# Moving value-tile copies ahead of the second head squares on ScalarE, with two loads and two VectorE steps in another order

## The reference

```python
for l in range(DEPTH):                     # DEPTH = 2
    mod = silu(c) @ w_ada[l] + b_ada[l]    # six rows of 1024: shifts, scales, gates
    h = rms_norm(x, norm_mix[l]) * (1 + sc1) + sh1
    gq, gk, gv, ga, gr, sq, sk, sv, mix_a, mix_b = split_columns(h @ w_in[l])
    y_gla = gla_branch(gq, gk, gv, ga, gr, ...) @ w_up_gla[l]
    y_swa = swa_branch(sq, sk, sv, ...) @ w_up_swa[l]
    x = x + g1 * ((sigmoid(mix_a) * y_gla + sigmoid(mix_b) * y_swa) @ w_out[l])
    h2 = rms_norm(x, norm_ffn[l]) * (1 + sc2) + sh2
    x = x + g2 * moe_ffn(h2, w_router, b_router, w_gate[l], w_up[l], w_down[l])

# in swa_branch: each head of q and k is normalised over its 64 numbers, then rotated
q = partial_rope(rms_norm(q, qn_gain), positions)
k = partial_rope(rms_norm(k, kn_gain), positions)
# in gla_branch: decays from a low-rank product; v is used as it comes out of the projection
log_a = log_sigmoid(a_low @ w_alpha2 + b_alpha) / GLA_TAU
```

## Time and profile before

| | |
|---|---|
| profiled execution | 1449.55 us |
| its span, first to last instruction | 1447.9 us |
| median of three runs | 1445.5 us |
| PE busy | 1342.6 us, 93% |
| PEld busy | 1079.4 us, 75% |
| DVE busy | 1032.0 us, 71% |
| ACT busy | 723.7 us, 50% |
| POOL busy | 312.9 us, 22% |
| chain that ended last, by engine | PE 72%, DVE 10%, DMA 7%, DVEq 4%, ACT 4% |
| mean granted TensorE clock | 0.974 of full |

### The profile page before, as it was taken

The page is one execution under the profiler, slowest core; times in us unless marked ns, Lnnn a source line. Parts: engine busy times, 40 slices in busy tenths (PEclk is TensorE's granted clock), DMA queues, the critical chain, the costliest instruction groups (busy, mean ns, idle before and its releaser), DMA issues.

```text
span 1447.9 us, 18728 instructions
## 1 busy us (share of the span) xinstructions
PE 1342.6 (93%) x6887; PEld 1079.4 (75%) x6888; DVE 1032.0 (71%) x1035; ACT 723.7 (50%) x770; POOL 312.9 (22%) x263
## 2 busy tenths in 40 slices
PE   4979999999999999999949999999999999999993
PEld 3756777786777888888748787688788788888682
DVE  5476476667477999999981558543548999999494
ACT  5225255222236777777652536522225777777370
POOL 1000000000214444555220000000022444454130
PEclk9999999999999999999979999999999999999997
DMA  9565602677677999999842230212356899999575
GB/s 333 200 235 188 243 1 73 210 284 250 232 291 250 372 383 387 389 376 380 310 138 69 107 109 9 74 62 113 121 206 244 291 369 372 373 374 388 211 262 194
DMA packets 157546, 342.96 MB, mean 237 GB/s; under 512 B 16998, under 2 KB 19258, under 8 KB 157474
## 3 DMA queue, kind: packets, MB, share of 16 engines
q1 hardware_dynamic: 139280, 316.82, 60.4%
q0 software_dynamic: 16304, 25.05, 4.8%
q10 hardware_dynamic: 1890, 0.15, 0.1%
HBM read 351.73 MB, written 23.63 MB: 259 GB/s over the span
## 4 chain that ended last, share of the span: by engine, by line
PE 72%; DVE 10%; DMA 7%; DVEq 4%; ACT 4%; issue 1%; ACTq 0%; SPq 0%; POOLq 0%
PE PS L1254 13%; PE PS L1256 12%; PE PS L1255 12%; PE PS L1668 8%; PE PS L1672 8%; PE PS L1662 8%; DMA ring<-in_w_ada 3%; ACT reg L1003 2%; PE PS L1650 2%; DVE reg L1863 2%; PE PS L1182 2%; DVEq L2181 1%; DVE ring_parts L1933 1%; DMA ring<-in_w_in 1%; DMA ring<-in_w_out 1%
## 5 line engine op out<-in xcount | busy, mean ns | idle before, releaser
L1254 PE MATMUL PS<-ring_parts 128*128 128x512 f32 (+1 forms) x704 | 276.9, 393 | 24.0 <-ACT reg L961 12.2
L2328 DVE TENSOR_TENSOR ring_parts<-ring,reg_parts 128x2048 fp32r<-128x2048 f32 x124 | 278.1, 2283 | 3.4 <-ACT reg_parts L1105 3.4
L1105 ACT ACTIVATE reg_parts<-ring 128x2048 fp32r<-128x2048 f32 x124 | 230.3, 1909 | 62.6 <-DMA ring<-in_w_down 38.3
L1933 DVE TENSOR_TENSOR ring_parts<-ring,ring_parts 128x2048 fp32r<-128x2048 f32 (+1 forms) x52 | 112.9, 2209 | 124.3 <-ACT ring_parts L925 124.2
L1254 PEld LDWEIGHTS PS<-ring_parts 128*128 128x128 f32 x704 | 134.2, 191 | 67.8 <-issue 31.7
L925 ACT ACTIVATE ring_parts<-ring 128x2048 fp32r<-128x2048 f32 (+1 forms) x52 | 93.4, 1846 | 159.3 <-DMA ring<-in_w_in 118.7
L2328 DVE TENSOR_TENSOR ring_parts<-ring,hT_parts 128x2048 fp32r<-128x2048 f32 x68 | 155.1, 2286 | 14.5 <-issue 13.2
L1255 PE MATMUL PS<-hT_parts,ring_parts 128*128 128x512 f32 x384 | 150.4, 392 | 0.0
L1256 PE MATMUL PS<-ring_parts 128*128 128x512 f32 x384 | 150.2, 391 | 0.0
L1105 ACT ACTIVATE hT_parts<-ring 128x2048 fp32r<-128x2048 f32 x68 | 126.5, 1909 | 25.4 <-DMA ring<-in_w_gate 19.4
L1672 PE MATMUL PS<-ring_parts,reg_parts 128*128 128x512 f32 x528 | 130.6, 389 | 0.0
(11 more groups left out here) (337 smaller groups left out, 2406.2 us busy)
## 6 DMA issues: line engine op xcount, KB each, us to landing
ring<-in_w_up SPq DMA_DIRECT2D x32, 2048.0 KB, 17.1
ring<-in_w_gate SPq DMA_DIRECT2D x32, 2048.0 KB, 12.2
ring<-in_w_down SPq DMA_DIRECT2D x32, 2048.0 KB, 18.7
ring<-in_w_ada SPq DMA_DIRECT2D x40, 1024.0 KB, 6.1
ring<-in_w_in SPq DMA_DIRECT2D x16, 2048.0 KB, 7.9
ring<-in_w_out SPq DMA_DIRECT2D x4, 2048.0 KB, 8.8
reg<-y_rows SPq DMA_DIRECT2D x16, 512.0 KB, 6.2
ring<-in_w_ada SPq DMA_DIRECT2D x3, 2048.0 KB, 17.2
```

What stands on the lines that cost most here:

```text
L1105: act.activation(high[:, cols], ring[:, 3 * k + part, cols], ACT.Copy).then_inc(w_hi[part], 1)
L1254: pe.matmul(out_, left[0], right[0], start=first, stop=False)
L1933: tt(ring_r[:, unit_slot(n), cols], w, ring_r[:, 2 + n % 2, cols].bitcast(F32), ALU.subtract).then_inc(lo_done, 1)
L2328: tt(ring_r[:, 3 * k + part, cols], ring[:, 3 * k + part, cols], high[:, cols].bitcast(F32), ALU.subtract).then_inc(w_lo[part], 1)
```

## The change

In both layers ScalarE squares the first two token tiles, copies the four value tiles, squares the second two, copies `aT`, and takes the root after that. In layer 0 VectorE sums half 6 ahead of the key unit's low part, and half 7 between the two reductions; in layer 1 there are no sums, and the reductions stand as before. The key unit's load is issued ahead of halves 4 and 5 in layer 0.

```diff
-    IN_HALVES, IN_BEHIND = (2, 4, 2, 4, 4), (2, 2, 0, 1, 1)
+    IN_HALVES, IN_BEHIND = (2, 4, 2, 4, 4), (2, 4, 0, 1, 1)
...
                 act.drain()
-                for i in range(2):
-                    if i == 1:
-                        act.wait_ge(qss_done, at(qss_done, l, 1))
+
+                def square_heads(i):
                     act.activation(sqt, qk[:, 2 * i:2 * i + 2, :, :].rearrange("p t h d -> p (t h d)"), ACT.Square).then_inc(qsq_done, 1)
-                act.wait_ge(qss_done, at(qss_done, l, 2))
-                act.activation(qss[:, :, :], qss[:, :, :], ACT.Sqrt, scale=1.0 / HD, bias=eps).then_inc(qsq_done, 1)
+
+                square_heads(0)
                 for t in range(NT):
                     act.wait_ge(v_ready, at(v_ready, l, t + 1))
                     act.activation(v[:, t, :], PS[:, in_bank(Q_V + t), :], ACT.Copy).then_inc(v_done, 1)
+                act.wait_ge(qss_done, at(qss_done, l, 1))
+                square_heads(1)
                 act.wait_ge(a_ready, at(a_ready, l, 1))
                 act.activation(aT, PS[0:GLA_RANK, in_bank(Q_A), :], ACT.Copy).then_inc(a_done, 1)
+                act.wait_ge(qss_done, at(qss_done, l, 2))
+                act.activation(qss[:, :, :], qss[:, :, :], ACT.Sqrt, scale=1.0 / HD, bias=eps).then_inc(qsq_done, 1)
                 split_high(4)
...
                 sum_own(0, 1)
                 split_low(2)
-                sum_own(2, 3, 4, 5)
+                sum_own(2, 3, 4, 5, 6)
                 split_low(3)
-                sum_own(6, 7)
-
-
-                for i in range(2):
+
+                def sum_head_squares(i):
                     dve.wait_ge(qsq_done, at(qsq_done, l, i + 1))
                     dve.tensor_reduce(qss[:, 2 * i:2 * i + 2, :], sqt.rearrange("p (t h d) -> p t h d", t=2, h=NN), AX.X, ALU.add).then_inc(qss_done, 1)
+
+                sum_head_squares(0)
+                sum_own(7)
+                sum_head_squares(1)
                 dve.wait_ge(qsq_done, at(qsq_done, l, 3))
                 dve.reciprocal(qss[:, :, :], qss[:, :, :])
```

## The result

The changed kernel took 1439.52 us (median of 17 runs, 1436.15 to 1443.89), beside 1447.7 us for the kernel before in its 17 runs (1445.24 to 1452.43). The ratio is 0.9938, with a 95% interval of 0.9926 to 0.9950: by the ratio 9.0 us faster, between 7.2 and 10.7, and by the two medians 8.2 us. The forecast was 1434.7 us with a range up to 1438.5, so the time lies 1.0 us above the range. The direction is right. The gain is smaller than the 10.8 us forecast, and the kernel before itself now stands 2.2 us above the 1445.5 that the forecast started from.

What follows compares the result with a forecast made beforehand. TensorE, busy 93% of the span, was taken as the bound, with a 12.2 us layer 0 wait for ScalarE's value copies. Saving 10.8 us there and 0 in layer 1 took 1445.5 to 1434.7 us, range 1432.0 to 1438.5.

Steps and rivals of the forecast that it cites:

- What bounds: Layer 0: TensorE's 12.2 us wait for ScalarE's value copies goes, and the key unit's low part is late next.
- When the low part is ready: VectorE, layer 0: key unit's low part ends at 102.0, so TensorE's first key tile starts after a 2.8 us gap.
- the unit's landing: Layer 0 key unit's load: asked for at 76.0, lands 7.76 us later, at about 83.8.
- The fixed delay: Loads of the halves: 2.5 us of fixed delay on top of about 2.6 us of transfer for 1 MB.
- A gap of 2.8 us is shorter than both, so I take full speed.: First key tile, layer 0: gap below the 4.9 and 3.5 us preceding earlier clock falls, so the tile takes 5.7 us.
- the first rival: Clock falls in the short gap before layer 0's first key tile: price 1.4 us, giving 1436.1 us; chance 8%.
- The sum: Whole kernel: -10.8 us in layer 0 and 0 in layer 1, from 1445.5 to 1434.7 us.
- the bound of 100.3: Layer 0: low part's end if transfers share and the unit does not delay the halves; gain 12.5 us.
- The order of the queue: SyncE's loads, layer 0: served in ring order, key unit first in full, half 4 landing at 86.4 rather than 84.7.
- W_R and the decay products: Layer 0: W_R lands at 117.0 as before; TensorE's second W_R tile keeps 2.8 us of margin behind the decay product.
- Layer 1: Reciprocal 6.6 us later, but L2001 already waited 3.91 us for ScalarE; cost nothing, with 0.5 us to spare.
- The level: Absolute starting time: the difference was taken from the median of 1445.5 us, not the profiled execution's 1449.55.

Runs made afterwards that it cites:

- gap_filled_14: Changed kernel with 14 spare 128x128 products in TensorE's gap ahead of layer 0's first key tile; ratio to the kernel before 0.9923.
- queue_undone: Changed kernel with the key unit asked for behind halves 4 and 5, as before; ratio to the kernel before 0.9946.
- half4_held: Changed kernel with SyncE waiting in layer 0 until the key unit has landed before issuing half 4; ratio to the kernel before 0.9933.
- act_only: Kernel before with ScalarE's new order alone, queue and VectorE order as before; ratio to the kernel before 0.9956.
- change_again: The changed kernel run once more, unaltered, as a gauge of run-to-run time; ratio to the kernel before 0.9921.
- sums_undone: Changed kernel with VectorE's order as before: low part behind half 5, halves 6 and 7, then both reductions; ratio to the kernel before 0.9918.
- halves_later_15: half6_behind with TensorE taking halves 8 to 14 one tile later in layer 0, half 15 with 14 behind the third gate tile; median 1435.1 us, ratio 0.9905.
- half6_behind: Changed kernel with half 6 summed behind the key unit's low part and the first reduction; ratio to the kernel before 0.9942.
- half6_behind_filled: half6_behind with 14 spare products in TensorE's wait for half 8; ratio to the kernel before 0.9928.
- gap_filled: Changed kernel with 26 spare 128x128 products in TensorE's gap ahead of layer 0's first key tile; ratio to the kernel before 0.9956.

## Why the prediction was wrong

- **What bounds.** Right. The value copies no longer hold TensorE; the low part is late next; removing half 6 from in front of it removed the wait.
- **When the low part is ready.** Mis-sized by 1.1 us. Counted from W_V's issue I had 39.5 and it was 40.7. The term that failed is the unit's landing: 7.76 us from a single row, against 9.0. The fixed delay and 2.6 us for a megabyte, the sums of 3.0 and 3.2 us, half 6's landing (5.0 us instead of 5.1) and the low part's 4.49 held. The gap was 4.0 us instead of 2.8.
- **"A gap of 2.8 us is shorter than both, so I take full speed."** This step failed, and it is the first rival, given 8%, that came, with the gap of nearly 4 us that it named. The clock fell and the tile took 7.3 us instead of 5.7: 1.6 us (gap_filled_14). The reasoning was faulty beyond the size. I compared the length of the gap with the time from the last matmul to the fall, but in the changed kernel the fall came 4.9 us after the last matmul, as in the earlier trace rows, when the gap was already over. Nor is that time fixed: it was 2.3 us in queue_undone, 2.7 in half4_held, 3.2 in act_only and 4.6 in change_again. act_only and sums_undone show falls behind waits of 2.5 and 1.8 us. What a gap of just 2.8 us with a full tile behind it would have done, no run shows. The Trainium skill, page "TensorE: Matmul & The Clock Gate", section "HAM oscillation — how this bites in real kernels", describes waits for loads behind which the matmuls start at the slow clock. The trace agrees with that for the wait of 4.0 us. The waits of its example are longer than 2.8 us, so the page alone did not decide the step; the runs do.
- **The sum.** 10.8 less 1.1 and less 1.6 is 8.1, and the stretch gained 8.05. The total's interval of 7.2 to 10.7 holds this and just excludes 10.8. Two small slips of the working change nothing: the bound of 100.3 and half a microsecond of spread give 1432.5, not 1432.0, and the key unit's own 2 MB took 5.3 us of its 10.26, not 5.4.
- **The order of the queue.** The rule of the Trainium skill, page "DMA: Bandwidth & Descriptors", section "Queues, rings and completion order", was the side I took. The trace agrees: half 4, issued 3.5 us behind the unit, landed 2.7 us behind it and 8.25 us after its own issue, where it took 5.1 with nothing ahead of it.
- **W_R and the decay products.** Right in effect. W_R took 11.5 us to land instead of 10.3 and, counted from W_V's issue, landed 2.8 us later than I had it. The decay product ended at 137.1 and TensorE's second gate tile began at 140.3, without a wait. The margin of 3.1 us was no thinner than the 2.8 forecast only because TensorE came 2.7 us later as well; halves_later_15, where TensorE is earlier, waits here.
- **Layer 1.** Right:

```profile
807.51 0.40 DVE L1974 RECIPROCAL qss<-qss 128x40 f32<-128x40 f32 x1 [0.40 <-ACT qss L966]
...
822.61 1.23 DVE L2006 TENSOR_TENSOR reg<-reg 128x1024 f32<-128x1024 f32 x1 [0.91 <-ACT reg L977]
```

  L2006 still waits for ScalarE, 0.9 us instead of the 3.9 of the earlier trace rows.
- **The level.** I took the difference from a median of three runs. Over 17 runs the same kernel's median was 2.2 us higher, and in the three other sets of its runs it was 1448.7, 1448.8 and 1450.0. Either error alone would have left the time inside: 1447.7 - 10.8 is 1436.9, and 1445.5 - 8.05 is 1437.5. Both together put it at 1439.5. The profiled execution of before at 1449.55 us had shown that single runs spread by 4 us.

## What to carry to other kernels

When an edit shortens a wait of TensorE but leaves one of 2 to 4 us, price the wait and the lower clock that can follow it, and look at what stands behind it: a full tile lost 1.6 us (2.2 in queue_undone), narrow products and then a tile lost 3.6 and 4.8. Filling the gap with spare products, or moving the late consumer one tile back, brought the causal products here to 98.4 and 95.5 us; moving the wait from one engine's list to another's left them at 99.9 to 102.6. Take the landing time of a load from several rows, and count an absolute forecast's range from the spread of runs, not from a median of three.

## What the runs showed of the hardware

- The granted clock fell at waits of TensorE of 1.8 us (sums_undone), 2.5 (act_only), 3.3 (half6_behind), 4.0 (changed kernel), 4.4 (queue_undone) and 6.4 (half4_held). It was low for 6.6, 10.2, 10.2, 3.6, 6.6 and 6.6 us between 96 and 126. In the first three the wait was followed by products of 32 columns of weights and of a depth of 16, and the clock came back only within the tile behind them; in the other three a full tile followed at once, and the clock came back within it.
- The time from TensorE's last matmul to the fall was 2.3 us (queue_undone), 2.7 (half4_held), 3.2 (act_only), 3.7 (sums_undone), 4.1 (half6_behind), 4.6 (change_again) and 4.9 (changed kernel). Two waits of the same 4.36 us had their fall 0.2 us after TensorE resumed (change_again) and 2.1 us before (queue_undone). What sets this was not tested.
- Filling the wait with 14 products of 128x128 kept it full in both kernels where 14 were tried (gap_filled_14, half6_behind_filled), and 26 did so in gap_filled. One such product took 0.23 us (14 products, 28 records, in 3.29 us).
- Two profiled executions of one and the same kernel differed by 8.3 us in span, 3.2 of them before the first edited load. The granted clock was at the lower level for about 9 us more in the slower one, which is at most 4.5 us of it; what makes the rest was not settled.
- A load of 2 MB with nothing beside it landed in 8.8 us in one place and in 7.8 in another; the longer one moved its last bytes for 1.2 us at a share of 0.07 of the 16 DMA engines (half4_held, 83.6 to 84.8).
